# Attention of a hybrid layer on one core: value products with tokens on the partitions, and TensorE walking the tile steps two at a time

## What is computed

```python
def mix(q_blk, k, v, mask):                       # per head, 512 queries x 512 keys, causal
    p = masked_softmax(einsum(q_blk, k) * scale, mask)
    return einsum(p, v)                           # 64 columns per head
# 8 NSA heads: three branches each, weighted by sigmoid gates of the token
o_a = g0 * o_cmp + g1 * o_slc + g2 * o_win        # cmp: 31 compressed keys
# 8 MLA heads: one branch, queries and keys of width 96, values of width 64
o_b = mix(q, k, v, causal)
mixed = concat([rmsnorm(o_a, out_gain_a), rmsnorm(o_b, out_gain_b)]) @ w_out
h = x + mixed
```

## Time and profile before

| | |
|---|---|
| median of 3 runs | 2412.17 us |
| the profiled execution's own time | 2410.7 us |
| its span, first to last instruction | 2408.7 us |
| granted TensorE clock, mean | 0.997 |
| TensorE matmul busy | 2372.0 us (98%) |
| VectorE / ScalarE / GpSimd busy | 1720.4 / 837.2 / 1115.0 us |
| attention, first scores to last scores | 968.3 to 1119.9 us of the span |

### The profile page before, as it was taken

How to read it: one execution, slowest core, us unless ns; L and a number is a source line. 1 busy time by engine, 2 the same in 40 slices (tenths; PEclk the granted TensorE clock), 3 DMA queues, 4 the chain that set the end, 5 groups by cost and what they waited for, 6 DMA issues and landing times.

```text
span 2408.7 us, 35086 instructions
## 1 busy us (share of the span) xinstructions
PE 2372.0 (98%) x12248; PEld 2033.5 (84%) x12248; DVE 1720.4 (71%) x2873; ACT 837.2 (35%) x1445; POOL 1115.0 (46%) x747
## 2 busy tenths in 40 slices
PE   8999999999999999899999999999999999999999
PEld 6888888878888887676889999999999888888887
DVE  8888785463433656876627699798886788888887
ACT  4132222100113315776224333344443333333333
POOL 7777776665666550103563788731112322222220
PEclk9999999999999999899999999999999999999999
DMA  4333323333332223100224899999999999999995
GB/s 158 97 105 105 104 95 126 134 111 108 132 117 95 88 74 121 36 1 10 70 88 127 286 311 303 301 354 347 339 342 402 383 356 349 353 358 354 346 359 200
DMA packets 181333, 490.41 MB, mean 204 GB/s; under 512 B 14848, under 2 KB 80512, under 8 KB 181248
## 3 DMA queue, kind: packets, MB, share of 16 engines
q1 hardware_dynamic: 144384, 355.12, 43.3%
q0 software_dynamic: 36864, 134.23, 14.9%
HBM read 436.86 MB, written 52.43 MB: 203 GB/s over the span
## 4 chain that ended last, share of the span: by engine, by line
PE 90%; issue 3%; POOL 3%; DVE 2%; ACT 1%; DMA 0%; SPq 0%; DVEq 0%; POOLq 0%; ACTq 0%
PE ps L690 40%; PE ps L1299 22%; PE ps L1259 17%; POOL spl L2661 2%; PE ps L1135 2%; PE ps L1280 2%; PE ps L1109 1%; POOL rare L2671 1%; PE ps L1094 1%; PE ps L874 1%; PE ps L1048 1%; PE ps L994 1%; PE ps L894 0%; PE ps L1098 0%; PE ps L1097 0%
## 5 line engine op out<-in xcount | busy, mean ns | idle before, releaser
L690 PE MATMUL ps<-hh,spl 128*128 128x512 f32 x1728 | 536.3, 390 | 4.3 <-DVE hl L2315 2.8
L1259 PE MATMUL ps<-hh,spl 128*128 128x384 f32 x2048 | 535.6, 337 | 2.9 <-POOL spl L2661 2.9
L1299 PE MATMUL ps<-spl,wsp 128*128 128x512 f32 x2304 | 523.8, 389 | 0.0
L1651 ACT ACTIVATE spl<-ring 128x1024 fp32r<-128x1024 f32 x256 | 271.9, 1062 | 678.0 <-PE ps L1299 325.6
L1299 PEld LDWEIGHTS ps<-spl,wsp 128*128 128x128 f32 x2304 | 432.0, 188 | 89.4
L2534 POOL TENSOR_TENSOR spl<-ring,spl 128x1024 fp32r<-128x1024 f32 (+1 forms) x164 | 425.6, 2595 | 13.1
L690 PEld LDWEIGHTS ps<-hh,spl 128*128 128x128 f32 x1728 | 324.3, 188 | 74.0 <-DVE hl L2315 4.2
L1259 PEld LDWEIGHTS ps<-hh,spl 128*128 128x128 f32 x2048 | 371.2, 188 | 6.3 <-issue 5.4
L2532 POOL CAST spl<-ring 128x1024 fp32r<-128x1024 f32 (+1 forms) x164 | 190.0, 1159 | 353.2 <-PE ps L690 334.6
L1259 PE MATMUL ps<-hl,spl 128*128 128x384 f32 x1024 | 342.5, 334 | 0.0
L2433 DVE TENSOR_TENSOR spl<-ring,spl 128x1024 fp32r<-128x1024 f32 x192 | 235.2, 1225 | 148.2 <-ACT spl L1651 134.3
(11 more groups left out here) (451 smaller groups left out, 3401.5 us busy)
## 6 DMA issues: line engine op xcount, KB each, us to landing
ring<-stream_in SPq DMA_DIRECT2D x134, 512.0 KB
ring<-u_in SPq DMA_DIRECT2D x128, 512.0 KB
ring<-v_in SPq DMA_DIRECT2D x128, 512.0 KB
ring<-stream_in SPq DMA_DIRECT2D x60, 704.0 KB
gelu<-gst SPq DMA_DIRECT2D x128, 192.0 KB
dense<-stage SPq DMA_DIRECT2D x12, 2048.0 KB
gl<-gelu SPq DMA_DIRECT2D x32, 768.0 KB, 7.1
gw<-dense SPq DMA_DIRECT2D x32, 768.0 KB, 9.9
```

The costliest lines, as they stand in the source:

```text
L690: m = pe.matmul(ps[:, bank, :], w[:, part, k0 + k * n:k0 + k * n + P], rhs(k), start=first and k == 0 and part == 0 and rhs is high, stop= ...
L1259: m = pe.matmul(ps[:, bank, 0:TD], w[:, part, k0 + k * P:k0 + (k + 1) * P], rhs(k), start=first and k == 0 and part == 0 and rhs is high, ...
L1299: m = pe.matmul(ps[:, bank, :], wsp[:, j % 2, part, tok], spl[:, j % 2, row, cols], start=False, stop=last and n == 2)
L1651: eng.activation(spl[:, j % 2, 0, 0:D], ring[:, j % RING, 0:D], ACT.Copy).then_inc(hi_done, 1)
```

## The change

All in the attention. The value products now have the turned probabilities as stationary operand (128 keys x 128 queries) and the values moving (64 columns), so that the output has tokens on the partitions: `values` (L1161), per step, one matmul for each of its qt+1 key tiles. For `cmp` it is one matmul of 256 columns (L1153). The probabilities are no longer scaled. Instead `weigh_head` (VectorE, L2298 to L2309) multiplies a finished branch's 128 x 256 output by gate over row sum, and adds it to the head's for `slc` and `win`. Evacuations of transposes go to VectorE for query tiles 0 and 1 and `cmp` (`evacuate_turned`, L2318), to ScalarE for the rest (L1633). The norm's squares move from GpSimd to ScalarE (`o_squares_of`, L1640), which takes the row sums along. The output is turned back by `turned_chunk` (TensorE, L1167), a matmul with a diagonal of the norm's inverse roots, so no rows are cast; high and low parts come straight from PSUM (`part_high` on ScalarE, `part_low` on VectorE). The first three score steps are issued among the `cast` groups, and their maxima among `head_scaled`. TensorE's loop takes two steps at a time.

```diff
-        vcz = [hnt[:, t // 3, (1 + t % 3) * P:(2 + t % 3) * P] for t in range(TT)]
-        HEAD_STEPS = [(SLC, 0), (SLC, 1), (CMP, 0), (SLC, 2), (SLC, 3), (WIN, 0), (WIN, 1), (WIN, 2), (WIN, 3)]
+        vcz = hnt[:, 0, :].rearrange("p (t c) -> p t c", t=TT)
+        HEAD_STEPS = [(SLC, 0), (SLC, 1), (SLC, 2), (SLC, 3), (CMP, 0), (WIN, 0), (WIN, 1), (WIN, 2), (WIN, 3)]
...
+        def on_dve(u):
+
+            return GROUPS[STEPS[u][0]][1] == "cmp" or STEPS[u][1] < 2
...
+        TURN_LAG, VALUE_LAG, WEIGH_LAG, EARLY = 2, 4, 9, 3
+        A_SQUARES, A_ROOT = A_H * PER + 6, A_H * PER + 10
+        A_TURNS = [A_H * PER + 13 + 4 * k for k in range(TT)]
...
+                    if HEAD_OF[n] == 0:
+                        pe.wait_ge(mid_ready, 1)
...
-            def output(n, kt):
-
+            def values(u):
+
+                n, qt = STEPS[u]
...
-                    if head >= 2 and kind != "win":
-                        pe.wait_ge(at_out, head - 1)
+                out_, turned = region(n), pt[:, u % TT, :]
+                pe.wait_ge(*evacuated(u))
...
-                        return
-                    if head == 0:
+                    if HEAD_OF[n] == 0:
...
-                    else:
-                        c = (kind == "win") * P
-                        v = vtok[:, kt, c:c + P]
...
+                            v = vm[:, kt, at * B_V:(at + 1) * B_V]
+                        else:
+                            c = (kind == "win") * P + g * A_D
+                            v = vtok[:, kt, c:c + A_D]
+                        m = pe.matmul(out_[:, qt, :], turned[:, kt * P:(kt + 1) * P], v, start=kt == 0, stop=kt == qt)
+                m.then_inc(at_pv, 1)
+
+            def turned_chunk(c, bank):

                 for t in range(TT):
-                    m = pe.matmul(ps[:, 0, P + t:P + t + 1], sqo[:, rows, t * P:(t + 1) * P], ones[:, 0:1], start=True, stop=True)
-                m.then_inc(sum_done, 1)
...
-                    pe.wait_ge(at_exp, u + 1)
-                    o_rows([ps[:, 1, 2 * P:3 * P]], TT - 1)
+            for u in range(0, NS, 2):
+                pe.wait_ge(at_exp, u + 2)
                 if u + TT < NS:
                     scores(*STEPS[u + TT])
-                elif u in FIRST_HALVES:
-                    first_half(FIRST_HALVES.index(u))
-                for n, kt in VALUES_AT.get(u, ()):
-                    output(n, kt)
-                if u < NS:
-                    turn(*STEPS[u])
+                    scores(*STEPS[u + TT + 1])
+                if u >= VALUE_LAG:
+                    values(u - VALUE_LAG)
+                    values(u - VALUE_LAG + 1)
+                for w in (u, u + 1):
+                    turn(w)
+                    if w in A_TURNS:
+                        c = A_TURNS.index(w)
+                        if c == 0:
+                            pe.wait_ge(inverse_done, 5)
+                        pe.wait_ge(*slot_user(turn_slot(w, True) - 2))
+                        turned_chunk(c, turn_bank(w, True))
+            values(NS - 4)
+            values(NS - 3)
+            values(NS - 2)
+            first_half(0)
+            values(NS - 1)
+            first_half(1)
             first_half(2)
-            pe.wait_ge(o_sum, 3)
-            o_column(1)
+            pe.wait_ge(inverse_done, 6)
+            for c, bank in zip(range(TT, DC), (0, 5, 6, 7)):
+                turned_chunk(c, bank)
             first_half(3)
-            pe.wait_ge(inverse_done, 6)
...
+            def o_squares_of(k, a, b, at=0):
+
+                t = k % TT
+                if k:
+                    eng.wait_ge(o_squares, min(k, 2 * TT))
+                eng.activation(weighted_sq[:, at:at + b - a], oall[:, (k >= TT) * TT + t, a:b], ACT.Square,
+                               accum_out=NORM_SUMS[k // TT][:, t:t + 1]).then_inc(o_squares, 1)
...
-                eng.wait_ge(o_ready, c + 1)
-                eng.activation(hh[:, c, :], oall[:, c, :], ACT.Copy).then_inc(mix_high, 1)
+                if u >= TURN_LAG and not on_dve(u - TURN_LAG):
+                    turned(u - TURN_LAG)
+                if A_SQUARES <= u < A_SQUARES + TT:
+                    eng.wait_ge(at_weighed, A_DONE)
+                    o_squares_of(u - A_SQUARES, 0, T)
+                elif u == A_ROOT:
+                    eng.wait_ge(o_squares, TT)
+                    o_inverse_root(NORM_SUMS[0])
+                elif u - 1 in A_TURNS:
+                    c = A_TURNS.index(u - 1)
+                    part_high(c, turn_bank(u - 1, True), a_parts[c][0])
+                elif u >= NS - 2:
+                    eng.wait_ge(at_weighed, A_DONE + B_EARLY)
+                    o_squares_of(TT + u - (NS - 2), 0, early)
+            eng.activation(rn[:, 1, 1:2], zero[:, :], ACT.Sqrt)
+            eng.wait_ge(at_weighed, B_DONE)
+            for t in range(TT):
+                o_squares_of(2 * TT + t, early, T, t * P)
+            eng.wait_ge(o_sum, 1)
+            o_inverse_root(NORM_SUMS[1])
+            for c, bank in zip(range(TT, DC), (0, 5, 6, 7)):
+                part_high(c, bank, hh[:, c, :])
...
+            early_bias(0)
             inverse(slice(R_KC, R_KC + 1), 4, A_G * N_CMP)
-            for h in range(4, B_H):
-                head_scaled(h)
+            head_scaled(4)
+            early_bias(1)
+            head_scaled(5)
+            head_scaled(6)
+            early_bias(2)
+            head_scaled(7)
...
+            def weigh_head(n):
+
+                g, kind, at = GROUPS[n]
+                total, part = totals[:, 0, n % 8, :], totals[:, 1, n % 8, :]
+                out_, tmp = head_rows(n), weighted[:, WEIGHED[n] % 2, :, :]
+                every_column = part.unsqueeze(2).to_broadcast([P, TT, A_D])
+                dve.wait_ge(at_exp, END_OF[n] + 1)
+                if kind == "cmp":
+                    step(dve.tensor_scalar(total, total, 1e-20, None, ALU.max))
+                step(dve.reciprocal(part, total))
+                if kind != "mla":
+                    col = 2 * P + (g * A_R + at) * 3 + ("cmp", "slc", "win").index(kind)
+                    step(dve.tensor_tensor(part, part, vtok[:, :, col:col + 1].rearrange("p t c -> p (t c)"), ALU.mult))
+                dve.wait_ge(at_pv, END_OF[n] + 1)
+                if kind in ("cmp", "mla"):
+                    dve.tensor_tensor(out_, region(n), every_column, ALU.mult).then_inc(at_weighed, 1)
...
+                    step(dve.tensor_tensor(tmp, region(n), every_column, ALU.mult))
+                    dve.wait_ge(at_weighed, WEIGHED[n] - 1)
+                    dve.tensor_tensor(out_, out_, tmp, ALU.add).then_inc(at_weighed, 1)
...
+            def evacuate_turned(u):
...
+                dve.tensor_copy(pt[:, u % TT, 0:nk], ps[:, turn_bank(u), 0:nk]).then_inc(at_ev_dve, 1)
...
-                if u < NS:
+                step(dve.reciprocal(rn[:, 0, :], rn[:, 0, :]))
+                for t in range(TT):
+                    m = dve.tensor_scalar(turned_by[:, t, :], cc("ident"), rn[:, 0, t:t + 1], None, ALU.mult)
+                m.then_inc(inverse_done, 1)
...
+            for u in range(NS + WEIGH_LAG - 1):
+                if EARLY <= u < NS:
                     top = step.mark(tops(*STEPS[u]))
-                if u >= LAG:
-                    inverse_at = step.mark(inverses(*STEPS[u - LAG]))
-                if u < NS:
+                if 0 <= u - TT - 1 < NS and on_dve(u - TT - 1):
+                    evacuate_turned(u - TT - 1)
+                if EARLY <= u < NS:
                     step.meet(top)
                     biases(*STEPS[u])
-                if u >= LAG:
-                    step.meet(inverse_at)
-                    shares(*STEPS[u - LAG])
-                if u == COLUMN_A + TT + 1:
+                for n in END_AT.get(u - WEIGH_LAG, ()):
+                    weigh_head(n)
+                if u == A_INVERSE:
                     o_inverted(1)
-                elif u in SCALED_A:
-                    o_scaled(SCALED_A.index(u), rstd[:, :]).then_inc(o_ready, 1)
+                elif u - TT - 1 in A_TURNS:
+                    c = A_TURNS.index(u - TT - 1)
+                    part_low(c, turn_bank(u - TT - 1, True), a_parts[c][1], a_parts[c][0])
...
+            weigh_head(GN - 1)
+            dve.wait_ge(o_squares, 3 * TT)
+            dve.tensor_tensor(NORM_SUMS[1], NORM_SUMS[1], NORM_SUMS[2], ALU.add).then_inc(o_sum, 1)
             o_inverted(2)
...
-                    if c == 2:
-                        pool.wait_ge(at_out, 1)
-                    else:
-                        tile_squares(0, 0, True)
-                        for tile in range(1, 3):
-                            step(tile_squares(tile, 0, False))
-                        tile_squares(3, 0, False).then_inc(o_sum, 1)
-                        pool.wait_ge(o_sum, 1)
+                    pool.wait_ge(at_weighed, 3 if c == 2 else A_DONE)
```

(40 more changed lines are left out.)

281 lines of the change are left out of this document (84 added, 197 removed).

## The result

The changed kernel takes 2484.88 us (median of 4 runs, 2478.11 to 2491.69), the kernel before 2412.32 in the same session. The ratio is 1.0299, 95% interval [1.0265, 1.0333]. It is slower by 72.6 us where the forecast was 2404, a gain of 8. The profiled execution took 2491.32 us with a span of 2489.4 and a mean granted clock of 0.970 (0.997 before).

A forecast was written before the change was run, and what follows sets the result against it. TensorE, with work in 98% of the span, was taken to bound the kernel. Terms of -5 (NSA heads), -4 (start), +2 (MLA heads) and -1 (behind the last scores) gave -8 us from 2412.17, so 2404 us; range 2393 to 2415.

The forecast's parts named there:

- the pair rival: Slower case: TensorE waits 52 times for both exponentials of a pair; over 4.8 us slower from 0.25 us each; chance 0.14.
- the term of the seven NSA heads: Seven NSA heads: value products save 4.8 us, pair waits replace present idle; -5 us, bounds -9 and +2.
- -8 + 52 s: Whole kernel: forecast sum if TensorE's wait for a pair's exponentials overruns by s each time; 2422 us at 0.35.
- 0.9 us of slack in the mean: Pair wait: TensorE's two pairs less the scores leave 4.4 us, against a chain of 3.5 us.
- if transposes or scores wait at most pairs for the exponential: Sign in the profile after, at TensorE's pairs, that the forecast is wrong.
- if the clock stays low beyond 981 us: Sign in the profile after, past the attention's start, that the forecast is wrong.
- Start, -4: Attention's start: early scores and transposes without scaled probabilities win, VectorE's added work costs 2.0; -4 us, bounds 0 and -7.
- Value products: TensorE in the attention: 0.1125 us per narrow pass, 2.25 us per branch, saving 4.8 us (NSA) and 1.1 us (MLA).
- MLA heads, +2: Eight MLA heads: turning chunks +3.6, stall 1, less value products, column sums and row casts; +2 us.
- at 1 us (0 if the lead holds, 5 if wait and square root add up): MLA heads: stall of ScalarE's exponentials behind the norm's squares, priced at 1 us.
- Behind the last scores, -1: Last scores to second halves: chunks +3.6, other work less, idle 3.70 falling to about 0.9; -1 us, bounds -3 and +3.

The follow-up runs named there:

- act_pairs: The changed kernel with ScalarE doing both exponentials of a pair before the evacuations, squares and high parts that stood between them: 2413.36 us, ratio 1.0000.
- pairs_early: The kernel before with TensorE's loop in pairs and the first two scores, with their maxima and biases, among the casts: 2408.27 us, ratio 0.9986.
- act_ends: act_pairs with six added 256-column passes ahead of only the first four pairs and the last: 2406.33 us, ratio 0.9984.
- one_step: The changed kernel with TensorE's loop taken one step at a time again, waiting for one exponential: 2419.55 us, ratio 1.0027.
- before_pairs: The kernel before with only TensorE's loop changed to pairs; wide value products, scaling and ScalarE's order as before: 2411.12 us, ratio 0.9986.
- act_fill: act_pairs with six added 256-column passes ahead of each pair: 2433.63 us, ratio 1.0091.
- evac_only: The changed kernel with only ScalarE's evacuations put behind both exponentials of a pair, the norm's operations at their old places: 2437.59 us, ratio 1.0086.
- fill: The changed kernel with six added 256-column passes ahead of each pair, overwritten by its scores: 2453.97 us, ratio 1.0168.

## Why the prediction was wrong

**The step that failed** is the pair rival, and with it the term of the seven NSA heads. The prediction had the right wait ("52 times TensorE waits for both exponentials of a pair"), the right formula (-8 + 52 s), and a wrong s. It put "two maxima (0.99), an evacuation (0.35) that itself waits for the transposes at the end of the earlier pair" into the chain and meant VectorE's evacuation. It never laid ScalarE's own queue beside TensorE's new order. There an evacuation waits for the end of the previous pair, and the second exponential stands behind it, at 23 of the 52 pairs by the order of the steps (the norm's operations do the same at six more), slack or not. "0.9 us of slack in the mean" was argued from lengths, but an in-order queue that needs the other's last instruction has no slack to share. Measured, s is 24.7 / 52 = 0.47 us in the mean (27 waits of 0.9), past the 0.25 from which that rival decides, and its formula gives -8 + 24.7 = +17, or 2429 us. The -5 for the NSA heads allowed 0.3 to 0.5 us a head for this wait; their scores waited 10.7 us, 1.5 a head.

**What no term of the prediction had** is the rest, 73 - 17 = 56 us in the median (64 in the profiled run). Most of it is the clock: 61 us by the estimate above, and act_pairs gets it back with the waits. The prediction looked for a low clock at the start only and named the rest as what would make it wrong. Two of its tests came true: "if transposes or scores wait at most pairs for the exponential" (at 27 of 52) and "if the clock stays low beyond 981 us".

**The other terms**, read in act_pairs and its relatives, where most of the waits are gone:

- *Start, -4:* right. 21.8 became 17.3 us, and the first transposes came at 971.74 us in the changed kernel where 971.5 was forecast. pairs_early shows that early scores (two of the three) do not win it alone. That the transposes without scaling do was not run by itself.
- *Value products:* right. Ten passes in 1.12 us (1092.31 to 1093.43 above), 0.112 each, the price taken from the earlier trace rows. The Trainium skill ("TensorE: Matmul & The Clock Gate", Back-to-back issue gap) gives about 81 ns per load and matmul of 128 columns; the trace has more for half the columns, so it disagrees.
- *Seven NSA heads, -5:* wrong apart from the waits. Its own terms add up to -5.2 to -6.6 (-4.8 for the values, and 0.3 to 0.5 us a head in place of 0.56), and the idle time from 960 to 1143.8 us is 15.2 us by the earlier trace rows, not 14; neither changes the verdict. At full clock act_ends needs 86.5 us against 88.6, so -2.1. The busy time of TensorE for two heads is 23.98 us, against 24.09 before: the work hardly fell.

Why not, the distances between starts show, added up over two heads by kind (act_ends 1021.6 to 1046.0, before 1022.0 to 1047.2, idle time left out): value products 9.86 against 11.30 us, -1.44 where the forecast had -1.36. But the 42 transpose passes take 5.13 us against 3.35. A row of each, before and act_ends:

```profile
1057.65 0.27 PE L1109 MATMUL ps<-cst,pr 128*128 128x128 f32 x1
1057.68 0.37 PE L1097 MATMUL ps<-kz,kq 128*128 128x256 f32 x1
```
```profile
1025.50 1.02 PE L1138 MATMUL ps<-cst,pr 128*128 128x128 f32 x7
1026.27 0.47 PE L1127 MATMUL ps<-kz,oah 128*128 128x512 f32 x1
```

From a single transpose between two other products to the next start it is 0.03 us; from seven in a row it is 0.77. Before, there are 18 groups in two heads; in act_ends nine. In the mean of the NSA heads a transpose pass takes 0.079 us before, 0.087 in one_step (groups as before, narrow products), 0.100 in before_pairs (groups as in act_ends, wide products), 0.094 in act_fill and 0.124 in act_ends. So grouping exposes the transposes' cost, by some 0.014 to 0.021 us a pass. I priced the value products alone and took the transposes as unchanged.

The larger part of the rise in act_ends is what is left of the pair wait. A group of three transposes in act_ends, in before_pairs and in act_fill:

```profile
1022.62 0.50 PE L1138 MATMUL ps<-cst,pr 128*128 128x128 f32 x3
1023.04 0.39 PE L1127 MATMUL ps<-kz,oah 128*128 128x256 f32 x1
```
```profile
1025.12 0.49 PE L1109 MATMUL ps<-cst,pr 128*128 128x128 f32 x3
1025.37 0.36 PE L1097 MATMUL ps<-kz,oah 128*128 128x256 f32 x1
```
```profile
1026.42 0.50 PE L1138 MATMUL ps<-cst,pr 128*128 128x128 f32 x3
1026.68 0.96 PE L1209 MATMUL ps<-kz 128*128 128x256 f32 x6
```

In act_ends the next scores start 0.42 us behind the group and not 0.25. They start at 1023.04, 0.05 us behind the end of the pair's second exponential (1022.99). The modelled end of the last transpose covers this wait, so the product's row shows none and TensorE counts as busy; the weight load of the same scores has it:

```profile
1023.04 0.19 PEld L1127 LDWEIGHTS ps<-kz,oah 128*128 128x128 f32 x1 [0.17 <-ACT pr L1628]
```

In act_fill the added passes stand in that place, and groups of three, five and seven take 0.25, 0.47 and 0.68 us. Taking act_fill's 0.094 as the price without such waits, they cost (0.122 - 0.094) x 42 = 1.2 us in two heads, some 4 us in seven (an estimate), and grouping alone some 2 us. Together that is 6 us, more than the 5 us that the value products save over seven heads.

- *MLA heads, +2:* right, +2.6 (52.3 against 49.7), once the squares are out of the exponentials' way. As written, the stall priced "at 1 us (0 if the lead holds, 5 if wait and square root add up)" cost some 24 us with the high parts and the clock: evac_only.
- *Behind the last scores, -1:* the order is right, since one_step has -1.6 and the second halves start without a wait for the low part. In act_pairs it is +3.2 because a pause of 0.97 us before the last values is followed by 0.50 of the clock; act_ends, without the fall, has 0.0.

The sum of the four forecast terms, -8, would have been -4.0 with most of the waits and the low clock gone (180.5 against 184.5, act_ends). But the added passes are no part of the change, and the kernel before still has its low clock at the start in this comparison (0.54 for 12.9 us). The change with only the waits gone (act_pairs) gives +2.6 over these marks and +1.1 in the medians, a tie.

## What to carry to other kernels

When one engine's order goes from single steps to pairs, write out the other engines' queues beside it, and for each instruction ask whether something ahead of it needs the *end* of the partner's group. Lengths and mean slack don't show this; an evacuation two steps behind instead of four cost 64 us in a kernel that was otherwise the old one in pairs. And price a regrouping by distances between starts over the whole loop, since a load that was hidden between other products can come out when the groups change.

## What was not expected of the hardware

Pauses that are 11% of the time, with narrow value products between them, went with a granted clock of 0.50 for 90 us on end. The same share of pauses, with the same narrow products in single steps (one_step's NSA heads), left it at 0.99. More than twice that share (33.0 of 131.2 us), with wide products, left it at 0.95. What decides between the three was not separated further. Added passes that compute nothing made the kernel 31 us faster in the one case (fill) and 7 us faster in the other (act_ends), by holding the clock up and filling waits. Even a kernel whose engine is 98% busy by the page should have its granted clock read stretch by stretch.
